# Where GpSimd makes the weights' low parts in the first attention: one step later, and a turned unit's low part ahead of the output's

## The reference

```
qkv = rmsnorm(x) @ w_qkv
A: 8 query heads of 64 (2 key heads), q and k normed and rotated:  softmax(q k^T / 8) v
B: 8 heads of 64, q and k rotated; three dilated windows merged:   softmax(q k^T / 8 + log count) v
x = x + rmsnorm(concat(out_a, out_b) @ w_out)
```

## Time and profile before

| | |
|---|---|
| median of the runs | 2027.71 us |
| time of the profiled execution | 2027.48 us |
| its span | 2025.7 us |
| busy share of the span: PE, DVE, ACT, POOL | 99%, 60%, 47%, 50% |
| granted clock of TensorE | 0.999 of full speed |
| chain that ended last: PE, DVE, POOL | 94%, 2%, 1% |

### The profile page before, as it was taken

One profiled execution on the slowest core, in us unless ns is written; L12 is line 12 of the kernel. 1 busy time (PEld: TensorE's weight loads), 2 busy tenths in 40 slices (PEclk: granted clock), 3 DMA queues, 4 the chain that ended last, 5 costly groups with the idle time before them and its releaser, 6 DMA issues.

```text
span 2025.7 us, 30460 instructions
## 1 busy us (share of the span) xinstructions
PE 2009.4 (99%) x11840; PEld 1750.0 (86%) x11840; DVE 1217.1 (60%) x1980; ACT 952.5 (47%) x1780; POOL 1019.0 (50%) x576
## 2 busy tenths in 40 slices
PE   9999999999999999999999999999999999999998
PEld 8999988877789999988888888899888888888997
DVE  6777731877738777812356573955333576568552
ACT  5455623567755444523444444444443545354443
POOL 4666643346753666644434443465534443264542
PEclk9999999999999999999999999999999999999999
DMA  6333332311133333323322222333332222223332
GB/s 189 106 107 107 102 100 94 122 52 48 48 107 112 105 105 105 104 94 107 117 84 73 73 83 73 94 104 103 107 130 85 83 74 73 84 84 94 105 114 73
DMA packets 245678, 193.67 MB, mean 96 GB/s; under 512 B 6944, under 2 KB 209184, under 8 KB 245152
## 3 DMA queue, kind: packets, MB, share of 16 engines
q1 hardware_dynamic: 245536, 191.73, 31.2%
HBM read 187.51 MB, written 2.10 MB: 94 GB/s over the span
## 4 chain that ended last, share of the span: by engine, by line
PE 94%; DVE 2%; ACT 1%; POOL 1%; issue 1%; SPq 1%; DMA 0%; ACTq 0%; DVEq 0%
PE bank L2231 20%; PE bank L2232 20%; PE bank L2233 20%; PE bank L2366 9%; PE bank L2364 9%; PE bank L2365 9%; PE bank L2225 3%; PE bank L2681 1%; PE bank L2523 1%; PE bank L2543 1%; PE bank L2550 1%; DVE x_tok L1463 1%; DVE xn L1458 0%; PE bank L2710 0%; PE bank L2712 0%
## 5 line engine op out<-in xcount | busy, mean ns | idle before, releaser
L714 POOL TENSOR_TENSOR w_lo<-w_raw,w_hi 128x1024 fp32r<-128x1024 f32 x216 | 533.5, 2481 | 463.2 <-ACT w_hi L874 461.5
L874 ACT ACTIVATE w_hi<-w_raw 128x1024 fp32r<-128x1024 f32 x271 | 283.1, 1054 | 197.6 <-DMA w_raw<-in_ffn_w_down 125.2
L2231 PE MATMUL bank<-xt_hi,w_hi 128*128 128x512 f32 (+1 forms) x640 | 243.6, 381 | 1.3 <-DVE xt_lo L1502 0.9
L2233 PE MATMUL bank<-xt_hi,w_lo 128*128 128x512 f32 (+1 forms) x640 | 239.3, 374 | 0.0
L2232 PE MATMUL bank<-xt_lo,w_hi 128*128 128x512 f32 (+1 forms) x640 | 239.3, 374 | 0.0
L2231 PE MATMUL bank<-w_hi,xt_hi 128*128 128x512 f32 (+1 forms) x456 | 178.3, 391 | 0.0
L2233 PE MATMUL bank<-w_hi,xt_lo 128*128 128x512 f32 (+1 forms) x456 | 174.4, 383 | 0.0
L2232 PE MATMUL bank<-w_lo,xt_hi 128*128 128x512 f32 (+1 forms) x456 | 174.3, 382 | 0.0
L2231 PEld LDWEIGHTS bank<-xt_hi,w_hi 128*128 128x128 f32 x640 | 120.5, 188 | 29.4 <-issue 5.3
L2233 PEld LDWEIGHTS bank<-xt_hi,w_lo 128*128 128x128 f32 x640 | 120.5, 188 | 21.9
L2232 PEld LDWEIGHTS bank<-xt_lo,w_hi 128*128 128x128 f32 x640 | 120.7, 189 | 19.6
(11 more groups left out here) (390 smaller groups left out, 5557.4 us busy)
## 6 DMA issues: line engine op xcount, KB each, us to landing
w_raw<-in_w_in SPq DMA_DIRECT2D x132, 512.0 KB, 3.8
w_raw<-in_ffn_w_down SPq DMA_DIRECT2D x44, 512.0 KB, 3.4
w_raw<-in_ffn_w_gate SPq DMA_DIRECT2D x43, 512.0 KB, 3.9
w_raw<-in_ffn_w_up SPq DMA_DIRECT2D x43, 512.0 KB, 3.8
w_raw<-in_w_out SPq DMA_DIRECT2D x24, 512.0 KB, 3.4
w_raw<-in_w_branch SPq DMA_DIRECT2D x24, 512.0 KB, 3.4
w_raw<-in_w_qkv SPq DMA_DIRECT2D x16, 512.0 KB, 3.9
x_tok<-in_x SPq DMA_DIRECT2D x4, 512.0 KB, 6.9
```

The costliest lines, as they stand in the source:

```text
L714: pool.tensor_tensor(lo_slots[i], raw_slots[i], f32(hi_slots[i]), ALU.subtract).then_inc(lo_ready, 1)
L874: act.activation(hi_slots[i], raw_slots[i], ACT.Copy).then_inc(hi_ready, 1)
L2231: pe.matmul(out_ap, ah, bh, start=first, stop=False)
L2233: return pe.matmul(out_ap, al, bh, start=False, stop=last)
```

## The change

Two things in GpSimd's loop. The low part of a slab moves from the steps with k modulo 3 = 1, which also have `unit_low`, to those with k modulo 3 = 2, which have only `normalise`; step 23 is left out, since it has a `unit_sum`. And `out_low` moves from ahead of `unit_sum` and `unit_low` to behind them.

```
             for k in range(-1, STEPS + 3):
                 if k + 1 < STEPS:
                     normalise(k + 1)
-                if k % 4 == 2 and k >= 6:
-                    out_low((k - 6) // 4)
                 if k % 3 == 0 and 0 < k // 3 < UNITS:
                     unit_sum(k // 3 - 1)
                 if k == 3 * UNITS - 1:
                     unit_sum(UNITS - 1)
                 if k % 3 == 1 and 0 < k // 3 < UNITS:
                     unit_low(k // 3 - 1)
                 if k == 3 * UNITS:
                     unit_low(UNITS - 1)
-                if k % 3 == 1 and k > 0:
+                if k % 4 == 2 and k >= 6:
+                    out_low((k - 6) // 4)
+                if k % 3 == 2 and k > 0 and k != 3 * UNITS - 1:
                     lows(done, slabs_cast(k))
                     done = slabs_cast(k)
```

## The result

The changed kernel takes 2031.54 us (median of 21 runs, 2030.43 to 2032.02), the kernel before beside it 2027.65 us (21 runs, most of them within 2027.4 to 2027.8). The ratio is 1.0018, 95% interval 1.0012 to 1.0024: a loss of 3.9 us by the medians, small but clear of the noise, and just within 0.2%. Forecast were 2029.7 and a range of 2027.5 to 2031.6.

The account below looks back on a forecast made before the run. TensorE, busy 99% of the span, was taken to bound the kernel, so reordering only opens or closes gaps. The terms -0.87 - 1.1 + 4.10 gave +2.1, forecast as 2029.7 us, range 2027.5 to 2031.6.

Parts of the forecast that it names:

- the pair: Step 26: step 22's slab joins step 25's, both ahead of `normalise(28)`; step 28 turns 4.10 us later, before gains come off.
- late landing of the swap: Step 23: unit 7's last swap lands in 3.8 us instead of 2.04, costing 0.5 us instead of gaining.
- Step 12: Slab goes behind `normalise(12)`, so TensorE starts earlier, next held by VectorE's low part: gain 0.87 us.
- Steps 22 to 24: `unit_low` ahead of `out_low` starts unit 7's swaps earlier, so step 24's values product comes earlier: gain 1.1 us.
- Unit 1's 2.3: Landing time in us assumed for unit 7's last swap, from unit 1's four swaps with the same spacing behind a slab.
- Is it given back behind?: Behind step 28: no later wait of TensorE in the stage could close, so the net 2.1 us loss stays.
- What I cost at nothing: Other moved slabs and `out_low` cost nothing; the tightest, step 14, leaves step 16 with 1.5 us of cover.
- Nothing at step 24: Step 24's 0.87 us wait on GpSimd adds no gain of its own, as the 1.51 us `o_sum` wait stands behind.
- Slower, since the gains don't reach the pair: Rival: a late swap landing at step 23 eats the gain there and costs 0.5 us; +3.7, or 2031.2 us; 12%.
- More than the pair: Rival: a loss elsewhere exceeds the 1.5 us of cover, as at step 16; about +3 us; 4%.
- Hidden: Rival: TensorE does not meet the two slabs ahead of step 28, so only gains of 2.6 us stand; 2024.9 us; 8%.

Follow-up runs that it names:

- e9: Kernel before with only the slabs of steps 22 and 25 paired in step 26, plus 19 added matmuls at step 28 and 8 at step 24: 2031.52 us.
- e10: Kernel before with only the slabs moved, `out_low` still ahead of the units, plus added matmuls, 8 at step 24 and 19 at step 28: 2030.60 us.
- e2: Kernel before with only `out_low` moved behind `unit_sum` and `unit_low`, slabs left in steps with k modulo 3 = 1: 2026.28 us.
- e3: Kernel before with only the slabs moved as in the change, pair included, `out_low` still ahead of the units: 2034.10 us.
- e4: Kernel before up to step 21, then the slabs of steps 22 and 25 together in step 26, the next in step 29: 2034.57 us.
- e7: Kernel before with only the slabs of steps 22 and 25 paired in step 26, plus 19 added matmuls in the wait at step 28: 2033.21 us.
- e5: Changed kernel plus 19 added matmuls, their result unread, in TensorE's long wait ahead of step 28's turnings: 2029.47 us.
- e1: Changed kernel without its pair: out-projection slabs 1, 2 and 3 go one each to steps 25, 28 and 31: 2025.22 us.
- e6: Changed kernel with the pair taken apart, slab 1 in step 25, slab 2 alone in step 26, slab 3 in step 29: 2028.47 us.
- e8: Changed kernel with the pair taken apart, one slab each in steps 25, 26 and 29, plus 9 added matmuls ahead of step 28: 2027.02 us.

## Why the prediction was right, and where it fell short

**Sign and mechanism: right.** The loss comes from the pair ahead of `normalise(28)`, in one wait of TensorE at step 28, forecast at 4.9 us and measured at 4.74. The signs came too: waits of 0.17 and 0.18 us on `pt_lo` at steps 12 and 24, a shorter one on `o_sum` (1.00 after 1.51, where 0.3 less was forecast), and 8.0 us idle in the stage.

**The size: too small, and the range held by luck.** Measured are +3.9 us at the median where +2.1 was forecast. The median lies 0.06 us inside the range, which reached that high for a late landing of the swap. In the changed kernel's profile that landing did not come, and what filled its place was a term that I did not have. My own band for the forecast, 2028.6 to 2030.6, does not hold the median, and it was added up wrongly: its terms give about 2028.9 to 2031.2, which does not hold it either.

**Step 12**, forecast -0.87, measured -0.90 (482.43 against 481.79 makes 0.64, the 0.17 of the stage's start come on top, and 0.1 for the shorter restart). VectorE's `pt_lo` is the next in line as said. e9 and e10 bear it out: e10 has the gain at step 12 and e9 has not, and they stand at +3.1 and +4.0.

**Steps 22 to 24**, a gain forecast at 1.1 us (at best 1.3, at worst a loss of 0.5), measured as 1.31 in the profile and 1.16 in e2. The four swaps started at 536.29, 0.87 us behind the slab as forecast (535.42 its issue), and took 2.9 to 2.0 us to land. Only the last counts, and it landed in 2.03. Unit 1's 2.3 was a little too dear, and the end at 2.04 that I had kept was the true one here. The 2.15 us that I had worked out from the Trainium skill, "DMA: Bandwidth & Descriptors", section "Anatomy of one DMA", was nearer than my row as well; that section is on DMAs that GpSimd issues, though, and SP issues these.

The late landing of 3.4 and 3.8 us did come, in e3 and e4, so not from the short spacing that I had feared: they start the swaps 2.14 us behind the slab. e7, e9 and e10 start them 2.16 us behind it and land the last in 2.03 or 2.04. In e4's trace one 16 KB packet of the queue for instructions runs in that stretch and two lone packets of the swaps follow it later. Such a packet alone is not enough to explain it: the kernel before has one between 541 and 542 us, with its last swap under way from 540.13, and lands it in 2.04. What makes the swap late stays open.

**The pair**, forecast +4.10, measured +3.97 in the profile and +4.0 in e9. The two slabs took 4.68 instead of 4.78 us.

**The sum of these** was +2.1; the profile has +1.76 and e5 +1.9. So the terms that I had were right to 0.4 us in all.

**The step that failed** is the one headed "Is it given back behind?", with its sentence that "the 2.1 us stay until the end". I asked what could be given back and not what a wait of 4.9 us, which I had just forecast, does to the engine that waits. In the profiled run TensorE's clock is at half for the first 3.1 us of work behind it. That is a missing term of 1.1 us in the profile (562.72 against 557.40 is 5.32, where the kernel before takes 4.18) and of 2.0 at the median of the runs, by e5. The trace before could not show it in this stage, where TensorE never stood more than 1.5 us. But it shows it at its end, where TensorE's last matmul is over at 2019.8 us and nothing follows (columns as in the earlier trace rows):

```profile
2020.00:2023.00 3.00, 0.00 (x0) 0.00 (x0) 1.41 (x3) 1.74 (x4) 0.00 (x0) 1.00 0.25 102
2024.00:2025.00 1.00, 0.00 (x0) 0.00 (x0) 0.00 (x0) 0.00 (x0) 0.00 (x0) 0.50 0.82 305
```

By 2024.0, which is 4.2 us behind the last matmul, the clock is at its lower level. A forecast wait of 4.9 us should have sent me there.

**What I cost at nothing**: the other steps held. Step 16, with its 1.5 us of cover, shows no wait in the changed kernel. "Nothing at step 24" holds for the change, but e3 and e4 show that it hung on `unit_low` coming first: removing one of two waits that stand close together lets the other grow by as much, and a gain of zero becomes a loss through the clock.

**The rivals.** "Slower, since the gains don't reach the pair" named the right size (+3.7) for a wrong reason: the gains were there. "More than the pair" was right that there was more, but looked for it at step 16 and not behind the pair's own wait. "Hidden" gave 2024.9; e1, which really hides the pair, is 2025.2.

## What to carry to other kernels

Where an engine is full, price a new wait twice: its length, and what its clock does after it. Here a wait of 4.7 us cost another 2.0, one of 2.4 us about 1.4 in most runs, and the waits up to 1.5 us in the profiled run of the kernel before none (two of that kernel's 21 runs are 1.4 and 1.6 us longer, and why is open). When a producer's side jobs are moved by a rule on the step number, list what the rule leaves out: the skipped step's job comes back with the next one, and two jobs of 2.4 us ahead of something urgent are worse than either, while 2.27 us of idle time stood unused one step before. And before taking away a short wait, look at the next one down the same queue: the two can join.

## What the runs showed that I had not expected

- A wait that the profile shows with full clock can still cost in the other runs: e6's profiled run had 1.00 behind its 2.45 us, and nine of its eleven runs were 1.3 to 2.5 us slower. A spread that widens, from e5's 0.3 to the change's 1.6 us, is the sign.
- The clock can fall after the wait is over: in e7 TensorE works again from 544.6, the granted clock is 1.00 up to 546, and only the stretch behind that has 0.53.
- Useless matmuls in a wait make a kernel faster: 2.0 us in e5, 1.4 in e8, 1.7 in e9, each pair taken against its own kernel before. They are no remedy, since e1 takes the wait away and is 4.1 us better than e5.
- Left open: what the one run in ten at +1.5 us is, which the kernel before has (2029.1), e9 and e10 too. In these sets e1, e2, e5 and e8 have none in eleven runs each.
